# Products of the unit matrix in five pauses of TensorE, and the second layer's gate columns taken out ahead of the splits, in a two-block transformer kernel

## The reference, cut to what matters

```python
y = y * jax.nn.silu(z['mla_gate'])
...
return mixed * pool_scale * jax.nn.silu(zz['pool_gate'])
```

```python
h = rmsnorm_2(x, norm_mix_pre[layer])
m = attention_mixer(...) if layer % 2 == 0 else recurrent_mixer(...)
x = x + rmsnorm_2(m, norm_mix_post[layer])
h = rmsnorm_2(x, norm_ffn_pre[layer])
x = x + rmsnorm_2(swiglu(h, ...), norm_ffn_post[layer])
```

## Time and profile before

| | |
|---|---|
| median of three runs | 1486.89 us |
| profiled execution, its own time | 1487.49 us |
| its span (first to last instruction) | 1485.7 us |
| mean granted TensorE clock | 0.986 |
| PE busy | 1424.4 us, 96% |
| DVE busy | 916.7 us, 62% |
| ACT busy | 734.1 us, 49% |
| POOL busy | 89.6 us, 6% |
| read from HBM | 209.98 MB, 142 GB/s over the span |

### The profile page before, as it was taken

One profiled execution on the slowest core, in us unless ns is written; L12 is line 12 of the kernel. 1 busy time (PEld: TensorE's weight loads), 2 busy tenths in 40 slices (PEclk: granted clock), 3 DMA queues, 4 the chain that ended last, 5 costly groups with the idle time before them and its releaser, 6 DMA issues.

```text
span 1485.7 us, 24078 instructions
## 1 busy us (share of the span) xinstructions
PE 1424.4 (96%) x10000; PEld 1243.7 (84%) x10000; DVE 916.7 (62%) x1536; ACT 734.1 (49%) x1186; POOL 89.6 (6%) x125
## 2 busy tenths in 40 slices
PE   5999999999999999999999989999999989999997
PEld 2666667888887775787999989889999989999997
DVE  4454765445454508586387668887676568967642
ACT  4433333623325335544455655686445468844442
POOL 0100000000000011000000010001221000012200
PEclk9999999999999999999999999999999999999998
DMA  9533331222223272332254565434666725366661
GB/s 319 173 113 114 101 112 44 75 82 85 74 83 114 85 284 102 128 100 72 86 171 156 188 231 171 130 115 164 191 197 217 237 74 183 128 199 195 190 193 48
DMA packets 65243, 212.59 MB, mean 143 GB/s; under 512 B 6704, under 2 KB 16176, under 8 KB 65136
## 3 DMA queue, kind: packets, MB, share of 16 engines
q1 hardware_dynamic: 63808, 205.29, 42.4%
q0 software_dynamic: 1328, 5.77, 1.1%
HBM read 209.98 MB, written 1.05 MB: 142 GB/s over the span
## 4 chain that ended last, share of the span: by engine, by line
PE 86%; DVE 7%; ACT 5%; issue 1%; DMA 1%; SPq 0%; POOL 0%; ACTq 0%; DVEq 0%; POOLq 0%
PE B L691 54%; PE B L1213 7%; PE B L898 3%; PE B L707 2%; DVE WL L2058 2%; PE B L708 2%; PE B L711 2%; ACT WH L1416 1%; PE B L1194 1%; PE B L976 1%; PE B L1224 1%; PE B L723 1%; PE B L847 1%; PE B L963 1%; PE B L848 1%
## 5 line engine op out<-in xcount | busy, mean ns | idle before, releaser
L2058 DVE TENSOR_TENSOR WL<-RAW,WH 128x1024 fp32r<-128x1024 f32 x336 | 409.3, 1227 | 278.8 <-ACT WH L1416 278.1
L691 PE MATMUL B<-XH,WH 128*128 128x256 f32 (+1 forms) x1584 | 499.5, 315 | 3.9 <-DVE ZG L2214 3.2
L691 PE MATMUL B<-XH,WL 128*128 128x256 f32 (+1 forms) x1584 | 484.1, 306 | 0.0
L691 PE MATMUL B<-XL,WH 128*128 128x256 f32 (+1 forms) x1584 | 483.9, 305 | 0.0
L1416 ACT ACTIVATE WH<-RAW 128x1024 fp32r<-128x1024 f32 x336 | 346.0, 1053 | 105.9 <-DMA RAW<-wstream 105.4
L691 PEld LDWEIGHTS B<-XH,WH 128*128 128x128 f32 x1584 | 297.9, 188 | 31.7 <-issue 8.0
L691 PEld LDWEIGHTS B<-XL,WH 128*128 128x128 f32 x1584 | 297.7, 188 | 21.1 <-issue 6.0
L691 PEld LDWEIGHTS B<-XH,WL 128*128 128x128 f32 x1584 | 297.6, 188 | 16.2
L1213 PE MATMUL B<-HH,WH 128*128 128x256 f32 x304 | 84.3, 277 | 0.0
L1213 PE MATMUL B<-HL,WH 128*128 128x256 f32 x304 | 84.3, 277 | 0.0
L1213 PE MATMUL B<-HH,WL 128*128 128x256 f32 x304 | 84.3, 277 | 0.0
(11 more groups left out here) (353 smaller groups left out, 2488.0 us busy)
## 6 DMA issues: line engine op xcount, KB each, us to landing
RAW<-wstream SPq DMA_DIRECT2D x368, 512.0 KB, 3.6
RAW<-wstream SPq DMA_DIRECT2D x32, 256.0 KB, 7.2
X<-x_t SPq DMA_DIRECT2D x4, 512.0 KB, 6.1
SW<-small POOLq DMA_DIRECT2D x2, 896.0 KB, 10.1
SW<-small POOLq DMA_DIRECT2D x2, 768.0 KB, 8.6
BT<-rel POOLq DMA_DIRECT2D x1, 1024.0 KB, 15.2
X<-consts POOLq DMA_DIRECT2D x1, 768.0 KB, 10.1
out_t<-X SPq DMA_DIRECT2D x3, 256.0 KB, 2.4
```

The costliest lines, as they stand in the source:

```text
L691: last = mm(out, w, x, start=i == 0, stop=i == len(pairs) - 1)
L2058: v.tensor_tensor(lo_of(h), raw_of(h), hi_of(h).bitcast(f32), ALU.subtract).then_inc(lo_ready, 1)
```

## The change

A new function puts products of the 128 x 128 unit matrix by itself into TensorE's queue; nothing reads what they write, and the next product that uses the bank starts it anew. It is called at five places: at the start of both layers of the first block (9 and 12 products) ahead of `first_rows`, in `pre_normed` of the attention and of the recurrence (10 each) ahead of the first round, and in the middle of the rounds of `rg_out` (9). The two calls of `pre_normed` for the feed-forward parts keep 0.

In the second layer of the first block, ScalarE and VectorE no longer split ahead between gate columns 0 and 1, and in the steps of columns 4 to 11 they take the gate column out first and split after it; the later call of `hi_upto` or `lo_upto` in the same step catches up to the same half. The first layer is unchanged in this.

```diff
+            def keep_busy(out, count):
+
+                for _ in range(count):
+                    mm(out[:, 0:P], ident, ident, start=True, stop=True)
+
...
                     outs.append(take(i, "z", l, b)[:, 0:ts.stop - ts.start])
+                keep_busy(outs[0], (9, 12)[l])
...
-            def pre_normed(k0, ring):
+            def pre_normed(k0, ring, busy=0):
 
                 outs = [take(banks.ring(ring))[:, 0:SEQ] for _ in range(3)]
+                keep_busy(outs[0], busy)
...
             def attention():
                 k0 = AT["stick_qk"]
-                pre_normed(k0, RING)
+                pre_normed(k0, RING, 10)
...
             def recurrence():
                 k0 = AT["rg_x"]
-                pre_normed(k0, RING)
+                pre_normed(k0, RING, 10)
...
                                        lambda kt: pe.wait_ge(y_lo, 1 + kt // 2)):
+                    if kt == KT // 2:
+                        keep_busy(BANK[4], 9)
                     pe.wait_ge(y_hi, 1 + kt // 2)
...
                 gate_block(0)
-                hi_upto(AT["g", l, 0] + lead)
+                if l == 0:
+                    hi_upto(AT["g", l, 0] + lead)
                 gate_block(1)
...
-                    if items:
+                    if items and (l == 0 or items[0][0] != "g"):
                         hi_upto(ahead(half_of(*items[0]), lead))
...
                 gate_block(0)
-                lo_upto(g0 + lead)
+                if l == 0:
+                    lo_upto(g0 + lead)
                 gate_block(1)
...
-                    if items:
+                    if items and (l == 0 or items[0][0] != "g"):
                         lo_upto(ahead(AT[items[0][0], l, items[0][1]], lead))
```

## The result

Time after: 1479.26 us median of 4 runs (1477.96 to 1481.23), beside 1487.0 (4 runs, 1484.94 to 1488.26) of the kernel before: ratio 0.9945, 95% interval 0.9925 to 0.9965. The forecast was 1478.0 with a range of 1474.5 to 1482.8. Both intervals exclude 1, and they overlap from 0.9947 to 0.9965, which is a gain of 5.2 to 7.9 us of 1487.

What follows compares the result with a forecast made beforehand. The prediction took TensorE, 86% of the span, to bound the kernel. Gains of 0 + 0.8 + 4.7 + 0.4 + 1.6 + 1.5 + 0.3 = 9.3 us from 1487.5 gave 1478.2, stated as 1478.0, range 1474.5 to 1482.8.

Steps and rivals of the forecast that it cites:

- Place 1: Start of the first block's first layer, nine unit products: gain 0, the next product waits for VectorE's low half.
- Places 2, 3, 4: Second layer's start, norm ahead of attention, norm ahead of recurrence: held clock gains 0.8, 1.6 and 1.5 us, limited by operands.
- Unit products: Batches in TensorE's pauses: 0.217 us per product, each batch done before the first real product's operand, so no cost.
- Gate columns 0 to 2: Second layer's block start: third value product runs at once, 1.4 us copy wait stays; gain 4.7 us, bounds 1.0 to 5.5.
- Gate columns 4 to 11: Second layer's later gate columns: bank free 1.4 us sooner, less about 1.0 lateness; gain 0.4 us, bounds -1.0 to 1.2.
- Place 5: Output of the recurrence, nine unit products: TensorE 1.7 us early, then waits on gapless VectorE; gain 0.3, at most 1.7.
- Sum: Whole kernel: 0 + 0.8 + 4.7 + 0.4 + 1.6 + 1.5 + 0.3 = 9.3 us gained.
- (a): Unit products do not hold the clock; only the gate columns pay, 5.1 us: 1482.4 us; chance 0.08.
- (b): VectorE absorbs the 4.7 us from the second layer's block start; 4.2 us gain is left: 1483.3 us; chance 0.10.
- (c): Cold stretches at the five places and value products pay in full, 15.4 us plus 0.9 of a pause: 1471.2; chance 0.06.
- (d): Unit products do not overlap, each instruction costs 0.28 us; 14.4 us on the path, less 9.3: 1492.6 us; chance 0.04.

Runs made afterwards that it cites:

- the second, 1480.6: The changed kernel, unaltered, measured again with 6 runs: median 1480.61 us, ratio 0.996 to the kernel before.
- the one profile with fewer: Changed kernel with 0, 6, 5, 2 and 4 unit products at the five places instead of 9, 12, 10, 10 and 9: 1481.46 us, one run.
- the one without falls in its profile: Changed kernel plus second-layer block-start splits spread out, recurrence-output sums behind last column, logits pairs apart, first layer's one unit earlier: 1476.37 us, 0.9928 to before.
- splits later: Changed kernel with ScalarE and VectorE splitting one column less ahead in the recurrence's output, catching up behind the seventh column: 1481.4 us, one run.

## Why the prediction was right

**Place 1 (0).** Right, -0.02; and without products it is 0 as well, with the fall. **Places 2, 3, 4 (0.8, 1.6, 1.5).** Measured 0.70, 1.54, 1.48. At place 2 the second round waits for ScalarE's upper half, as forecast. At place 3 the reason is shown: 0.85 us of lateness cost nothing, since VectorE's low halves pace the rounds. **Unit products (0.217 each, under cover).** 0.22 and no late first product.

**Gate columns 0 to 2 (4.7).** The mechanism is as written (third value product at once, then a wait of 1.4 for the copy); the size was 4.05. The term mis-sized is the run behind it: 0.86, 0.43, 0.86 and 0.86 for value, rotation, queries and keys make 3.0 us, and from 607.63 to the column's steady pace at 611.05 (610.66 + 0.68 - 0.28) it took 3.4. That and a start 0.1 later are 0.5 of the 0.65. That the 1.4 wait is safe for the clock was half luck: in two of nine profiles with this order it fell there and took 1.5 to 1.7 back. The forecast's lower bound for that case was a gain of 1.0; it was still 2.4 and 2.5.

**Gate columns 4 to 11 (0.4).** Wrong: nothing measured. The wait for the gate column did shrink, from 2.48 to 1.29. Around it came waits of 0.39, 0.36 and 0.72 us (they begin at 666.58, 667.59 and 677.84), and one of 0.72 that followed it before went. Taken by the starts of TensorE's products, 1.0 us is lost at 667, 1.2 gained back at 673, 0.9 lost at 679 and 0.6 gained at 680: the forecast weighed 1.4 from the earlier bank against 1.0 of lateness, and measured the two cancel. What the new order does do is to break one long wait, behind which the clock fell in two of four profiles; whether that spares falls is open.

**Place 5 (0.3).** The size was right (0.42), and that was luck, since the engine was wrong: "everything TensorE needs for the next stage follows on VectorE". What gives the gain back is TensorE's wait of 1.00 us for GpSimd, in the middle of the last column. Behind it was ScalarE, whose square, copy, upper half and split fill 2.13 us a column, and GpSimd's sum on its squares. The 0.27 us rest in the earlier trace rows was a wait for ScalarE; that row said so.

**Sum (9.3).** By profile 8.2, so 1.1 less: 0.65 at gate columns 0 to 2, 0.4 at the later ones, and 0.1 at places 2 to 4 that place 5 makes good. That accounts for 1.1 of the 1.3 us from 1478.0 to the first median, 1479.3. It does not account for the second, 1480.6, nor for the profiled run, 1481.23. That one has 1.41 us more than the kernel before in the fall at 252, which the diff doesn't touch and which lasts 3.41 or 6.83 us. The forecast took it as a constant, from one profile.

**Rivals.** (a) no: clock 1.00 behind every batch. (b) no: the 4.05 is still there at 727 (-2.99 from +1.35, with 0.3 of chance; -3.38 from +0.48 in the second profile, 3.9). (c) no. The Trainium skill, TensorE: Matmul & The Clock Gate, "HAM oscillation", multiplies the throttled time by (1 - 1.2/2.4). An estimate by that rule is 3.4 us for place 3 (6.82 us at half clock in the earlier trace rows), where 1.54 came: the clock alone sets an upper bound here. That the operands paced the rest is shown at places 3 and 4. (d) no: 0.22 a product.

## What to carry to other kernels

Products on data that is there, put into TensorE's own wait, cost nothing here as long as they ended before the operand, and four to six were enough in the one profile with fewer. What they return is set by the operand that is late next, not by the clock's ratio. The longest wait isn't the one to look at alone: list every stretch at half clock over several profiles, since the same kernel falls or doesn't, for 3.41 or 6.83 us, at half a dozen places, and much of its spread from run to run goes with that. In the last batch the kernel before ran from 1482.2 (mean granted clock 0.992) to 1491.3 us (0.985) in 11 runs, the one without falls in its profile from 1475.5 to 1477.0 (6 runs).

## What the runs showed of the hardware that was not expected

- A granted clock of 0.50 came while TensorE was busy without a pause: 250.60 to 257.43 in after has 6.83 of 6.83 us busy, behind some 4 us of transposes, scores and 16-row products and a wait of 0.74. It came at another place when those products were set apart, and not at all when dense columns followed each pair; which of the products and the wait matters isn't shown.
- A wait of 2.03 us with two unit products ahead of it let the clock fall, waits of 1.36 to 1.65 us with four to six ahead of them did not, and one of 1.38 at the block start, among short products, did in two of nine, and one of 2.47 or 2.48 later in the block in two of four. The same wait of the same kernel can go either way, so one profile says little.
- GpSimd and VectorE slow each other. VectorE's low half of M (L2550 in after, ML) takes 0.47 to 0.49 us by itself and 1.50 to 1.57 four times in every profile, each time beside one of GpSimd's additions: in after 1.52 at 1274.22 and 1.51 at 1278.33. Where the two overlap by 0.3 us or less it keeps its 0.48. In splits later one of 0.49 falls wholly into GpSimd's first addition of the sum, and it is the addition that takes longer: 2.99 us in the place of 1.65 in after, the same instruction on the same data. No run takes one of the two away.
